# Attention streams: ScalarE copies the transposed probabilities in two parts, and the product with V begins after the first three blocks

## The reference

```python
sc = jnp.einsum("bshd,bmhd->bhsm", q, k).astype(jnp.float32) * scale
p = jax.nn.softmax(sc, axis=-1)
o = jnp.einsum("bhsm,bmhd->bshd", p, v.astype(jnp.float32)).astype(h.dtype)
```

## Time and profile before

| | |
|---|---|
| time of three runs | 4191.66, 4196.93, 4202.71 us; median 4196.93 us |
| the profiled execution | 4192.77 us, span 4191.0 us |
| mean granted TensorE clock | 0.953 |
| PE busy | 3848.7 us (92%) |
| PEld busy | 3214.3 us (77%) |
| DVE busy | 2189.9 us (52%) |
| ACT busy | 1267.4 us (30%) |
| POOL busy | 1223.3 us (29%) |

### The profile page before, as it was taken

The page is one execution under the profiler, slowest core; times in us unless marked ns, Lnnn a source line. Parts: engine busy times, 40 slices in busy tenths (PEclk is TensorE's granted clock), DMA queues, the critical chain, the costliest instruction groups (busy, mean ns, idle before and its releaser), DMA issues. The chain is left out here.

```text
span 4191.0 us, 48720 instructions
## 1 busy us (share of the span) xinstructions
PE 3848.7 (92%) x19370; PEld 3214.3 (77%) x19370; DVE 2189.9 (52%) x3457; ACT 1267.4 (30%) x1971; POOL 1223.3 (29%) x548
## 2 busy tenths in 40 slices
PE   6999998899999999899998998899999879999998
PEld 4777876787767787777776786789999668876886
DVE  4456746886765575497886566331111555533113
ACT  3322234121332323421223444221111335543222
POOL 1233433343322343333431110122222200023442
PEclk9999999999999999999999998899999889999999
DMA  2123422444322343234441100112222100012332
GB/s 88 52 67 105 136 81 71 116 125 127 107 61 66 84 130 90 86 106 128 118 131 45 31 26 16 41 51 61 66 62 60 51 14 16 21 54 70 91 95 76
DMA packets 544399, 316.69 MB, mean 76 GB/s; under 512 B 35828, under 2 KB 517167, under 8 KB 544175
## 3 DMA queue, kind: packets, MB, share of 16 engines
q1 hardware_dynamic: 543903, 312.53, 26.0%
q10 hardware_dynamic: 272, 1.05, 0.1%
HBM read 311.44 MB, written 2.10 MB: 75 GB/s over the span
## 5 line engine op out<-in xcount | busy, mean ns | idle before, releaser
L447 POOL TENSOR_TENSOR wlo<-wraw,whi 128x1024 fp32r<-128x1024 f32 (+6 forms) x544 | 1223.1, 2256 | 2932.7 <-ACT whi L440 2932.3
L463 PE MATMUL acc<-hh,whi 128*128 128x512 f32 (+2 forms) x2744 | 1072.4, 391 | 62.0 <-DVE hl L620 28.2
L464 PE MATMUL acc<-hl,whi 128*128 128x512 f32 (+2 forms) x2744 | 1039.5, 379 | 0.0
L465 PE MATMUL acc<-hh,wlo 128*128 128x512 f32 (+2 forms) x2744 | 1038.6, 378 | 0.0
L440 ACT ACTIVATE whi<-wraw 128x1024 fp32r<-128x1024 f32 (+6 forms) x544 | 523.8, 965 | 895.1 <-DMA wraw<-in_w_up 389.5
L463 PEld LDWEIGHTS acc<-hh,whi 128*128 128x128 f32 x2744 | 524.7, 191 | 189.0 <-POOL wlo L447 37.3
L464 PEld LDWEIGHTS acc<-hl,whi 128*128 128x128 f32 x2744 | 524.9, 191 | 91.0 <-issue 12.7
L465 PEld LDWEIGHTS acc<-hh,wlo 128*128 128x128 f32 x2744 | 523.8, 191 | 85.4
L1466 DVE TENSOR_TENSOR t<-acc,sq 128x768 f32<-128x768 f32 (+1 forms) x44 | 36.3, 825 | 493.2 <-PE acc L465 493.2
L1310 DVE SCALAR_TENSOR_TENSOR sq<-ada_w,scT,sq 128x512 f32<-128x512 f32 x168 | 247.2, 1472 | 0.0
L463 PE MATMUL acc<-act1h,whi 128*128 128x512 f32 x528 | 213.7, 405 | 29.2 <-DVE act1l L1474 25.8
(11 more groups left out here) (370 smaller groups left out, 6111.5 us busy)
## 6 DMA issues: line engine op xcount, KB each, us to landing
wraw<-in_ffn_w SPq DMA_DIRECT2D x120, 512.0 KB, 3.8
wraw<-in_w_in SPq DMA_DIRECT2D x102, 512.0 KB, 3.9
ada_w<-in_ada_w SPq DMA_DIRECT2D x96, 512.0 KB, 4.1
wraw<-in_w_up SPq DMA_DIRECT2D x88, 512.0 KB, 5.5
wraw<-in_w_down SPq DMA_DIRECT2D x32, 512.0 KB, 5.5
wraw<-in_w_out SPq DMA_DIRECT2D x16, 512.0 KB, 4.0
wraw<-in_w_mkv SPq DMA_DIRECT2D x16, 512.0 KB, 4.0
wraw<-in_ab_w_in SPq DMA_DIRECT2D x14, 512.0 KB, 3.8
```

The costliest lines, as they stand in the source:

```text
L447: e.tensor_tensor(wlo[0:rows, s, a:b, 0:w], wraw[0:rows, s, a:b, 0:w], whi[0:rows, s, a:b, 0:w].bitcast(F32), ALU.subtract).then_inc(lo_re ...
L463: e.matmul(o, wh, xh, start=first, stop=False)
L464: e.matmul(o, wh, xl, start=False, stop=False)
L465: return e.matmul(o, wl, xh, start=False, stop=last)
```

## The change

ACT copies the first three blocks (384 columns) of the transposed probabilities and signals, then copies the rest and signals again. PE begins the product with V after the first signal and waits for the second before the fourth block. All counts of `s_copied` double. Instances with two blocks have one copy as before, which signals twice at once. 144 instances have more than three blocks and get the second copy.

```diff
+        COPIED_FIRST = 3
...
-                    e.wait_ge(s_copied, c.at(s_copied, n))
+                    e.wait_ge(s_copied, c.at(s_copied, 2 * n - 1))
                     e.wait_ge(ob_free[0], c.next(ob_free[0]))
                     copied(False)
                     slot["pv"] = n
                     for j, vj in enumerate(t["v"]):
+                        if j == COPIED_FIRST:
+                            e.wait_ge(s_copied, c.at(s_copied, 2 * n))
                         mm = e.matmul(ob[0][:, 0:t["dv"]], sq[:, 0, j * P:j * P + P], vj, start=j == 0,
                                       stop=j == len(t["v"]) - 1)
...
                     if n:
-                        e.wait_ge(s_copied, c.at(s_copied, n))
+                        e.wait_ge(s_copied, c.at(s_copied, 2 * n))
...
                     if n:
                         e.wait_ge(s_pv, c.at(s_pv, n))
-                    e.activation(sq[:, 0, 0:w], ptf[:, 0:w], ACT.Copy).then_inc(s_copied, 1)
+                    m = min(w, COPIED_FIRST * P)
+                    e.activation(sq[:, 0, 0:m], ptf[:, 0:m], ACT.Copy).then_inc(s_copied, 1 if m < w else 2)
+                    if m < w:
+                        e.activation(sq[:, 0, m:w], ptf[:, m:w], ACT.Copy).then_inc(s_copied, 1)
                     if n == N - 1:
-                        e.wait_ge(s_copied, c.next(s_copied, N))
+                        e.wait_ge(s_copied, c.next(s_copied, 2 * N))
                         e.sem_inc(pt_free, 1)
```

More of the change, by code:

```diff
@@ L935, in pe_flow @@
             c.keep("made", c0 + sum(j["kind"] in MAKES for j in jobs))
-            for sem_, k in ((s_nb, total), (s_probs, total), (s_comb, combs), (s_copied, N), (s_raw, raws), (s_full, fulls)):
+            for sem_, k in ((s_nb, total), (s_probs, total), (s_comb, combs), (s_copied, 2 * N), (s_raw, raws), (s_full, fulls)):
                 c.next(sem_, k)
```

## The result

The changed kernel takes 4169.19 us, the median of four runs from 4164.68 to 4172.91. The kernel before, run beside it, takes 4198.20 us (four runs, 4191.66 to 4202.71). The ratio is 0.9933, with a 95% interval of 0.9916 to 0.9950. The profiled execution took 4167.04 us at a mean granted TensorE clock of 0.960 (before: 4192.77 us at 0.953).

The account below looks back on a forecast made before the run. PE, busy 92% of the span, was taken as the bound, with time won only where it stands or its clock falls. Waits 10.1 us plus clock 1.6 us gave 11.7 us, so 4185 us against the median 4196.93; range 4177 to 4195.

Parts of the forecast that it names:

- The waits of MLA: MLA: 16 products with V start 0.312 us earlier each, after a 384-column copy instead of 768 columns.
- 28 x 0.312: Dilated attention's 12 and MLA's 16 counted waits, each 0.312 us shorter: 8.7 us.
- the six products that are just in time: MLA's tail: six products start 0.15 us after the last scores matmul; 0.03 us gained each, 0.2 us together.
- The waits of dilated attention: Dilated streams: 12 products, all after 1.3 us or more of idle weight loads, start 0.312 us earlier each.
- The second part and ACT: Second copy ends 0.38 us before PE wants it; ACT's extra 0.07 us per copy costs 0, at most 1.5 us.
- The added wait: PE's wait before the fourth block, 144 times: taken as 0, bound 27 us; as a slower rival, chance 0.08.
- Window attention: Seven five-block waits, one not counted; the six left gain 0.198 us each, 1.2 us together.
- The wait at 2379.69: Window attention: not counted, since PE would wait away at 2387.84 what it wins there.
- the 10.1 of the sum: All shorter waits together: 8.7 + 1.2 + 0.2 = 10.1 us.
- The clock: MLA: one of four falls to 1.2 GHz goes, 1.6 us (range 0 to 6.2); dilated streams either way 2 or 3.
- the clock follows: Rival: all four MLA falls go and one or two in other streams; 18 us gained, 4179 us; chance 0.20.
- The rival that the gain is taken back: Other waits replace the shortened ones or a fall is added; 4 us left, 4193; chance 0.27, shared with slow first copy.

Follow-up runs that it names:

- only the added wait: Against the kernel before: one whole copy that signals twice, with the wait before the fourth block kept; 4194.26 us, ratio 0.9993.
- the filled kernel: Against the kernel before: copy whole, four extra products with overwritten results before the wait in 14 MLA instances; 4188.26 us, ratio 0.9979.
- kernel with the dilated waits filled: Against the kernel before: copy whole, 5 to 11 extra products with overwritten results before 12 long waits in the dilated streams; 4187.50 us, ratio 0.9980.

## Why the prediction came out as it did

**The waits of MLA: right.** 0.312 us each had been forecast; the standing went from 1.05 to 0.73 and the period from 18.23 to 17.91. The terms were 5.0 us (16 of the 28 x 0.312) and 0.2 for the six products that are just in time; the waits gave 5.7. The list of waits has 4.9 of it. The rest is in the six products at the end, which follow each other after 3.00 us instead of 3.12: 0.12 each, where 0.03 had been forecast.

**The waits of dilated attention: right.** Twelve times 0.312 is 3.7 us. In the half stream three of the twelve give 1.0. The first long wait of the first and of the third stream fell by less, from 1.39 to 1.20 us and from 1.70 to 1.54, so that about 3.5 is reached.

**The second part and ACT: right.** It is in time by 0.38 us with three blocks; with two it is just late, and the loads take 0.04 us longer. No MLA period is longer for ACT's extra 0.06 us.

**The added wait: right.** I took 0 with a bound of 27 us; only the added wait gave 0.9993. The page of the Trainium skill that was cited (Advanced Engine Details and Errata, Network/Comms) would have made it 7 to 14 us by its 50 to 100 ns. No run here shows such a cost in a stream of weight loads, and the measurement decides.

**Window attention: somewhat too large, and one wait misread.** I had six times 0.198. Three of those waits, up to 2310, are shorter by about 0.22 each, but behind two of them PE stands longer ahead of a job's first load. Before:

```profile
2287.97 1.19 PEld L904 LDWEIGHTS ob<-vg,sq 128*128 128x128 f32 x10 [0.84 <-ACT sq L980]
...
2289.84 0.19 PEld L463 LDWEIGHTS ob<-hh,whi 128*128 128x128 f32 x1 [0.23 <-issue]
```

and in the kernel with only this stage split:

```profile
2295.38 1.19 PEld L907 LDWEIGHTS ob<-vg,sq 128*128 128x128 f32 x10 [0.62 <-ACT sq L984]
...
2296.44 0.59 PEld L924 LDWEIGHTS pt<-ident,t 128*128 128x128 f32 x5
...
2297.52 0.19 PEld L463 LDWEIGHTS ob<-hh,whi 128*128 128x128 f32 x1 [0.50 <-issue]
```

From the product to the job's load it was 1.87 us and is 2.14: the 0.22 us that the product won are given back. What the load waits for isn't in the row; the job's bank, which DVE sets free, is the likely one, but no run shows it. The wait at 2379.69 of the earlier trace rows had been left out, since PE would wait away at 2387.84 what it wins there. It did not: the first went from 2.09 to 1.87 us and the second only from 1.18 to 1.21, where it would have had to grow by 0.2, and from the product at 2374.50 to the one at 2392.19 it is 17.69 us before and 17.51 with this stage split. The pair is worth one wait, as in the sum, but it is the first that gives it. With the two later waits of 2.08 us, which fell to 1.87, 0.6 to 0.8 us of the 1.2 are reached. The shorter waits of all stages come to about 10 us, which is the 10.1 of the sum.

**The clock: the step that failed.** It read: "With 0.31 us less standing some of the four should go: none to all, 0 to 6.2 us. I take one, 1.6 us." All four went, in all six profiles of kernels whose product in MLA starts after the first part; and the term was too small in three ways. MLA without falls is 7 to 10 us shorter by the filled kernel, and 14 where there were seven long periods; the one trace at hand had four, the fewest of all, and a stretch at the stream's end also lost some (a period of 19.5 us or 21.1 with the whole copy, 19.3 with the split one). Dilated attention was to "move either way by 2 or 3 us"; by the two profiles of each kernel it gained 9 to 13 us in its windows, and the kernel with only this stage split is 13 to 15 us faster; the waits are about 3.5 of it, so 6 to 12 are clock. In the seven profiles whose dilated products wait for the whole copy, unfilled, the second stream of a layer ended at the lower clock in 12 of 14 cases; with the early start in none of 12, of which four are filled too. In the earlier trace rows the twelve loads take 2.63 us; where they do, PE's loads behind are 0.43 us apart instead of 0.23, and the price of a fall is that of all the work until the clock is back. After the change the same half stream reads:

```profile
314.30 1.42 PEld L907 LDWEIGHTS ob<-tails,sq 128*128 128x128 f32 x12 [1.28 <-ACT sq L984]
...
317.27 1.42 PEld L907 LDWEIGHTS ob<-tails,sq 128*128 128x128 f32 x12 [0.99 <-ACT sq L984]
320.06 1.41 PEld L907 LDWEIGHTS ob<-tails,sq 128*128 128x128 f32 x12 [0.82 <-ACT sq L984]
```

And window and differential attention, for which I had no clock term, gained 4.7 us.

By its effect the rival *the clock follows* was the case. It had 0.20 and 18 us; at its own words it was still too small, because it priced only MLA's four falls and 2 us elsewhere. What misled me was a count: "most waits were not followed by a fall", nine of thirteen. I read it as proof that a wait decides little. It is just as well in keeping with waits that are close to what decides, and then 0.31 us less of each can move all of them, as it did in MLA. The sum by the runs: the waits are 5.7 + 3.5 + 0.7, about 10 us, and the clock is the rest, 18 of the 28 us (20 of the 30 of the three stages), where the prediction had 1.6.

**The rival that the gain is taken back** is half true in one stage. In window and differential attention PE's busy time fell by 8.3 us and the span by 4.7. A wait of 1.21 us appears before 2462.24 that was not there while PE worked at 1.2 GHz (the first row is the kernel before, the second the changed one):

```profile
2473.96 1.31 PEld L904 LDWEIGHTS ob<-vg,sq 128*128 128x128 f32 x10
...
2462.24 1.19 PEld L907 LDWEIGHTS ob<-vg,sq 128*128 128x128 f32 x10 [1.21 <-ACT sq L984]
```

PE at the lower clock arrived later, when the copy was done. This is why the list of waits of this stage went up, from 18.0 to 19.4 us, while its time went down.

**Placing counts too in window and differential attention.** Two stretches show it, before and with only this stage split:

```profile
2445.44:2450.51 5.07, 5.07 (x26) 3.81 (x27) 1.06 (x6) 1.48 (x4) 0.00 (x0) 0.66 0.00 2
2463.83:2478.42 14.59, 14.59 (x89) 13.16 (x89) 4.98 (x20) 6.34 (x14) 2.37 (x1) 0.77 0.13 37
...
2452.68:2456.24 3.56, 3.56 (x26) 2.76 (x27) 1.06 (x6) 1.54 (x5) 0.00 (x0) 1.00 0.01 2
2469.36:2481.90 12.54, 11.77 (x90) 10.08 (x90) 5.50 (x20) 6.38 (x18) 2.36 (x1) 1.00 0.15 43
```

Ahead of the first stretch PE stands for 2.15 us in both kernels, and yet one falls behind it and the other does not. Ahead of the second it stands for 2.08 us before and 1.87 with the split. But in the kernel with MLA filled, whose copies are whole here, it stands for 2.14 us and keeps the clock:

```profile
2468.51:2481.01 12.50, 11.72 (x90) 10.08 (x90) 5.32 (x20) 5.99 (x14) 2.36 (x1) 1.00 0.15 43
```

That kernel loses more elsewhere, in the stretch 84 us later (14.60 us for the instructions that take 12.97 before), and its stage is no shorter, 343.5 us. So in this stage it is not shown that the shorter standing by itself did it: the split may as well have moved the work to where no fall came. What is shown is that the gain repeats, in all six profiles with the split here, 336.8 to 339.8 us.

**What stays open.** That the standing brings the clock down is shown for dilated attention and MLA, by filling it. In window and differential attention nothing was filled; that its 4 us come from the clock is read from the PEclk of its window (0.92 to 0.95, and the same with only this stage split). Why a given wait of 1.05 us is followed by a fall and the next isn't, and why kernels with the whole copy have four or five long periods or seven, also stays open. The 0.06 us longer standing of two kernels is no answer, since the two with the split elsewhere have 18.23 us in the short period and seven long ones as well.

## What to carry to other kernels

Where PE stands still for about a microsecond again and again, look at the granted clock behind each wait, and price the wait at its length plus what the slower matmuls behind it cost; here the second was nearly twice the first. A copy that the product waits for is worth cutting in two where the second part ends before the product reaches it; if the wait can't be shortened, try matmuls whose result is overwritten. When a fall follows some of many equal waits, reckon with it that a little less standing removes all of them, and test it in one stage at a time.

## What the runs showed of the hardware

- Extra matmuls in PE's waits made the kernel faster, ratio 0.9979. The short period of MLA stayed at 18.23 us, and the long ones near 19.8 us, with their lower granted clock, were gone.
- A satisfied semaphore wait between two matmuls of a product cost nothing: 144 of them, 4194.26 us, ratio 0.9993.
- An ACT copy from PSUM of 384 columns takes 0.47 to 0.49 us, of 256 columns 0.36, of 768 columns 0.80; two parts in a row overlap by 0.10 us, so that a split costs about 0.06 us.
- The order of waits ahead of a product matters a little: with the wait for the copy last of three, the product started 0.06 us later (1.11 us of standing instead of 1.05, kernel with the dilated waits filled).
- Window and differential attention took 343.1 to 343.7 us in all eight profiles whose products wait for the whole copy there, though the falls of the clock did not lie at the same places in all of them (clock 0.77 in the stretch from 2463.83 of the kernel before, 1.00 in the same stretch with MLA filled).
